# Feed-forward joins of a two-block fp32 kernel: longer tails in token halves, three tile pairs in halves, transposes ahead of the last run

## The reference

```python
h = h + rms_norm(mixed, mix_post_g)                 # mixed = (...) @ w_out          -> "out1"
u = rms_norm(h, ffn_pre_g)                          #                                -> x2
gt, up = split(u @ w_ffn_in)                        # 22 tiles of 128 each           -> g1, u1
h = h + rms_norm((silu(gt) * up) @ w_ffn_out, ffn_post_g)                        #   -> "ffn1"
# second block
x = x + rms_norm(mix @ w_out_2, attn_post_norm)     #                                -> "out2"
h = rms_norm(x, ffn_pre_norm)                       #                                -> x4
x = x + rms_norm(conv_ffn(h, gate, up, ..., down), ffn_post_norm)  # 32 tiles: g2, u2 -> "ffn2"
```

## Time and profile before

| | |
|---|---|
| median of 3 runs | 927.5 us |
| profiled execution | 927.46 us, span 925.7 us |
| TensorE busy | 903.5 us (98%) |
| weight loads, overlapping | 799.8 us (86%) |
| VectorE busy | 678.7 us (73%) |
| ScalarE busy | 465.2 us (50%) |
| GpSimd busy | 222.9 us (24%) |
| granted TensorE clock | full in every slice |

### The profile page before, as it was taken

The page is one execution under the profiler, slowest core; times in us unless marked ns, Lnnn a source line. Parts: engine busy times, 40 slices in busy tenths (PEclk is TensorE's granted clock), DMA queues, the critical chain, the costliest instruction groups (busy, mean ns, idle before and its releaser), DMA issues.

```text
span 925.7 us, 16815 instructions
## 1 busy us (share of the span) xinstructions
PE 903.5 (98%) x6767; PEld 799.8 (86%) x6767; DVE 678.7 (73%) x1274; ACT 465.2 (50%) x936; POOL 222.9 (24%) x120
## 2 busy tenths in 40 slices
PE   8999999999999999999999999999999999999997
PEld 7879999989999888888888799887888888888885
DVE  6924986658655888766676767867888888788885
ACT  6334336564443574434444646776734345544343
POOL 3523421441212211642314342221100211210121
PEclk9999999999999999999999999999999999999999
DMA  8454443234333655655545354224545455455531
GB/s 297 164 188 159 162 142 136 99 113 137 131 122 123 230 178 191 227 183 201 192 160 221 136 190 151 110 90 157 184 153 212 182 182 211 159 222 182 209 110 46
DMA packets 23181, 153.67 MB, mean 166 GB/s; under 512 B 2864, under 2 KB 3248, under 8 KB 5568
## 3 DMA queue, kind: packets, MB, share of 16 engines
q1 hardware_dynamic: 22384, 150.43, 45.9%
q0 software_dynamic: 576, 2.10, 0.6%
q10 hardware_dynamic: 144, 0.07, 0.0%
HBM read 151.28 MB, written 1.05 MB: 165 GB/s over the span
## 4 chain that ended last, share of the span: by engine, by line
PE 61%; DVE 25%; ACT 9%; issue 4%; DMA 0%; DVEq 0%; SPq 0%; ACTq 0%
PE pb L506 59%; DVE wl L515 10%; ACT wh L512 4%; DVE FA L515 4%; DVE FA L521 3%; ACT FA L512 3%; DVE FA L518 3%; PE pb L509 2%; DVE wh L530 1%; ACT R L512 1%; DVE X L521 1%; DVE R L521 1%; DVE st L518 0%; DMA X<-in_x 0%; DVE FA L524 0%
## 5 line engine op out<-in xcount | busy, mean ns | idle before, releaser
L506 PE MATMUL pb<-R,wh 128*128 128x256 f32 (+2 forms) x2224 | 551.5, 327 | 5.9 <-ACT R L512 2.0
L506 PE MATMUL pb<-R,wl 128*128 128x256 f32 (+1 forms) x1512 | 423.9, 282 | 0.0
L506 PEld LDWEIGHTS pb<-R,wh 128*128 128x128 f32 x2224 | 371.9, 189 | 46.4 <-ACT R L512 3.5
L515 POOL TENSOR_TENSOR wl<-raw,wh 128x1024 fp32r<-128x1024 f32 (+1 forms) x80 | 195.0, 2442 | 634.3 <-ACT wh L512 525.1
L515 DVE TENSOR_TENSOR wl<-raw,wh 128x1024 fp32r<-128x1024 f32 (+1 forms) x198 | 263.1, 1350 | 82.4 <-ACT wh L512 80.8
L506 PEld LDWEIGHTS pb<-R,wl 128*128 128x128 f32 x1512 | 286.2, 189 | 2.5 <-issue 0.6
L512 ACT ACTIVATE wh<-raw 128x1024 fp32r<-128x1024 f32 (+1 forms) x219 | 222.7, 1044 | 53.4 <-PE pb L506 51.5
L506 PE MATMUL pb<-wh,R 128*128 128x512 f32 (+2 forms) x724 | 235.0, 389 | 2.3 <-ACT R L512 1.0
L506 PEld LDWEIGHTS pb<-wh,R 128*128 128x128 f32 (+1 forms) x724 | 134.5, 187 | 35.4 <-ACT R L512 2.4
L512 ACT ACTIVATE FA<-pb 128x256 f32<-128x256 f32 (+7 forms) x240 | 94.1, 414 | 127.1 <-PE pb L506 116.0
L506 PE MATMUL pb<-wl,R 128*128 128x512 f32 (+2 forms) x372 | 144.4, 388 | 0.0
(11 more groups left out here) (122 smaller groups left out, 478.5 us busy)
## 6 DMA issues: line engine op xcount, KB each, us to landing
raw<-in_w SPq DMA_DIRECT2D x137, 1024.0 KB, 4.8
X<-in_x SPq DMA_DIRECT2D x2, 512.0 KB, 4.5
raw<-in_w SPq DMA_DIRECT2D x2, 512.0 KB, 6.3
post<-in_ffn_post SPq DMA_DIRECT2D x2, 512.0 KB, 4.5
post<-in_w POOLq DMA_DIRECT2D x2, 512.0 KB, 5.2
FA<-in_w POOLq DMA_DIRECT2D x2, 512.0 KB, 8.6
out<-X SPq DMA_DIRECT2D x4, 256.0 KB, 2.0
cst<-in_cst SPq DMA_DIRECT2D x1, 821.5 KB, 12.0
```

Source lines behind the costliest of these rows:

```text
L506: return self.real.matmul(*a, **k) if self.real else self
L515: return self.real.tensor_tensor(*a, **k) if self.real else self
```

## The change

Six things are changed together:

1. Tails: out1 and out2 sum their last five K blocks in token halves instead of four (`TAIL`). A tail of five runs three blocks for both column halves, then the last two for column half 0, then for column half 1.
2. `SPLIT_TILES` is 3: gate and up tiles 0, 1 and 2 go through `gemm0` and `gemm1`. The third pair takes the banks in `THIRD`.
3. The transposes of token half 0 (`turn`) stand before the tail's last run of half 1, by the new `MIX` strings of out1 and out2.
4. In x2 and x4 the transposes of token half 1 go to two banks, four in each, taken in the order 0, 4, 1, 5, 2, 6, 3, 7; an operand's high part waits for the low part two before it.
5. The wide places begin four units earlier (`opens = first - 4`): 80 to 83 and 176 to 179 are the opened ones. For out2 the splits behind 172 to 174 are issued in the join's own list.
6. `MADE` has other makers for 80, 82, 83, 84, 85, 87, 89 (now d, p, d, d, p, p, q) and 176, 178, 179, 181, 183, 184, 185 (now d, p, d, p, p, q, q).

```diff
-SPLIT_TILES = 2
+SPLIT_TILES = 3
+TAIL = dict(out1=5, ffn1=4, out2=5, ffn2=4)
...
     def down_tail(name, order):
...
-        units = p.weights(("tail", name), [(w, 128 * k, rng(128 * j)) for k in order[-4:] for j in range(8)])
-        return [[("tail", name, c, h)] for c in range(2) for h in range(2)], units
+        n = TAIL[name]
+        units = p.weights(("tail", name), [(w, 128 * k, rng(128 * j)) for k in order[-n:] for j in range(8)])
+        runs = [((0, 1), 0, n - 2), ((0,), n - 2, n), ((1,), n - 2, n)] if n > 4 else [((0,), 0, n), ((1,), 0, n)]
+        return [[("tail", name, c, *r)] for c in range(2) for r in runs], units
...
-        segs.append((down, main, [*chains(down, x), refill(units, list(range(first, first + NWIDE - NBASE)))]))
+        opens = first - (NWIDE - NBASE)
+        held = list(range(units[0] - 8 + TAIL[down], units[0])) if down == "out2" else []
+        segs.append((down, main, [*chains(down, x), refill(held + units, list(range(opens, first)))]))
...
-        return first
+        return opens
...
-MADE = (... "dpddpddvvdddqvddddpd" ... "pvdppvpppdvvdddvpdqddddd" ...)
+MADE = (... "ddddpddpdpqqddddpd" ... "pvdppvppddpddpdpqqqddddd" ...)
...
-    "out1": "............c.cac..aacbab.a.aa..bb.bcbbcc.c...",
+    "out1": "........cccc" "...." ".a.ac.acac.aaa.bbbb......bbbcc......",
...
-    "out2": "c.cac.a.a.aca.bcaa..bbc.bbcbbc....",
+    "out2": "cccccc" "." ".ac.ac.acac.aaa.bbbb......bbbcc......",
...
-        TURN = dict(x2=((4, 5, 0, 1), (6, 7, 4, 5)), x3=((4, 5, 0, 1), (6, 7, 4, 5)), x4=((0, 1, 4, 5), (2, 3, 0, 1)))
+        TURN = dict(x2=((4, 5, 0, 1), (6, 7)), x3=((4, 5, 0, 1), (6, 7, 4, 5)), x4=((0, 1, 4, 5), (2, 3)))
+        THIRD = dict(g1=(4, 5), u1=(4, 5), g2=(0, 1), u2=(0, 1))
...
+        def turns(x, c):
+
+            n = len(TURN[x][c])
+            at = [(k % 4, 128 * (k // 4)) if n == 4 else (k // 4, 128 * (k % 4)) for k in range(8)]
+            return [(k, *at[k]) for k in (range(8) if n == 4 else (0, 4, 1, 5, 2, 6, 3, 7))]
...
                 elif kind == "op":
                     x, c, i = a
-                    for j in range(4):
-                        k = 4 * i + j
+                    for z in range(4 * i, 4 * i + 4):
+                        k, j, at = turns(x, c)[z]
                         e.wait_ge(*pe.at(("turn", x, c, j)))
-                        if i:
-                            e.wait_ge(*dve.at((x, "l", j, c)))
+                        if z >= len(TURN[x][c]):
+                            e.wait_ge(*dve.at((x, "l", turns(x, c)[z - len(TURN[x][c])][0], c)))
```

More of the change, by code:

```diff
@@ L319, in ffn @@
         segs.append((None, p.take(), []))
-        return first
+        return opens
     for n in range(8):
         p.tile("yb", n)
-    for k in range(4):
+    for k in range(8 - TAIL["out1"]):
         p.wide(("down", "out1", k), "w_out", k, [rng(128 * j) for j in range(8)])
@@ L350, in segments @@
         p.tile("mk", n, True)
-    for k in range(4):
+    for k in range(8 - TAIL["out2"]):
         p.wide(("down", "out2", KORD2[k]), "w_out_2", KORD2[k], [rng(128 * j) for j in range(8)])
@@ L433 @@
 for _n, (_, _, _kt) in DOWN.items():
-    _ks = (KORD2 if _n == "out2" else list(range(_kt)))[-4:]
+    _ks = (KORD2 if _n == "out2" else list(range(_kt)))[-TAIL[_n]:]
     TAIL_AT.update({(_n, _k): BLOCK_AT["tail", _n] + 8 * _i for _i, _k in enumerate(_ks)})
@@ L925, in tensor @@
                     src = SRC[name][0]
-                    b = bank(("gemm", name, n), RINGA[name])
+                    b = bank(("gemm", name, n), THIRD[name] if n == 2 else RINGA[name])
                     both = b.rearrange("p (a t) -> p a t", a=2)[:, :, 0:128]
@@ L938, in tensor @@
                     b = banks.of(use)
+                    order = [k for k, _, _ in turns(src, 1)]
                     both = b.rearrange("p (a t) -> p a t", a=2)[:, :, 128:256]
-                    for k in range(8):
+                    for k in order:
                         u, o = divmod(BLOCK_AT["gemm", name, n, 0, 8] + k, 8)
@@ L1014, in tensor @@
                 elif kind == "tail":
[L1015 to L1019, removed]
+                    name, c, hs, k0, k1 = a
+                    ks = (KORD2 if name == "out2" else list(range(DOWN[name][2])))[-TAIL[name]:]
+                    for k in ks[k0:k1]:
+                        m, u = down(name, k, c, False, k == ks[-1], hs)
+                        names = [("used", u), ("down", name, k)] if c and hs[-1] else []
+                        names += [("tail", name, c, h) for h in hs] if k == ks[-1] else []
                         if names:
@@ L1194, in tensor @@
                     m_, = a
-                    b = bank(step, B5, True)
+                    b = bank(step, B4 if m_[0] == "moba" else B5, True)
                     PT, V = Tm(m_), MAPS[m_]["v"]
@@ L1296, in scalar @@
                     x, c, i = a
-                    for j in range(4):
-                        k = 4 * i + j
+                    for z in range(4 * i, 4 * i + 4):
+                        k, j, at = turns(x, c)[z]
                         e.wait_ge(*pe.at(("turn", x, c, j)))
-                        if i:
-                            e.wait_ge(*dve.at((x, "l", j, c)))
-                        e.activation(operand(x, k, 0)[:, 128 * c:128 * c + 128], banks.of(("turn", x, c, j))[:, 128 * i:128 * i + 128],
+                        if z >= len(TURN[x][c]):
+                            e.wait_ge(*dve.at((x, "l", turns(x, c)[z - len(TURN[x][c])][0], c)))
+                        e.activation(operand(x, k, 0)[:, 128 * c:128 * c + 128], banks.of(("turn", x, c, j))[:, at:at + 128],
                                      ACT.Identity, scale=sc(PRE_GAIN[x], k)).then_inc(*act.up((x, "h", k, c)))
@@ L1604, in vector @@
                     x, c, i = a
-                    for j in range(4):
-                        k = 4 * i + j
+                    for z in range(4 * i, 4 * i + 4):
+                        k, j, at = turns(x, c)[z]
                         t = slice(128 * c, 128 * c + 128)
                         e.wait_ge(*act.at((x, "h", k, c)))
-                        e.scalar_tensor_tensor(operand(x, k, 1)[:, t], banks.of(("turn", x, c, j))[:, 128 * i:128 * i + 128],
+                        e.scalar_tensor_tensor(operand(x, k, 1)[:, t], banks.of(("turn", x, c, j))[:, at:at + 128],
                                                sc(PRE_GAIN[x], k), rf(operand(x, k, 0)[:, t]), ALU.mult,
                                                ALU.subtract).then_inc(*dve.up((x, "l", k, c)))
-                        if i:
+                        if z >= 8 - len(TURN[x][c]):
                             banks.ended(("turn", x, c, j), dve.now())
```

15 lines of the change are left out of this document (8 added, 7 removed).

## The result

The changed kernel takes 946.16 us (median of six, 944.89 to 948.03), beside it the kernel before 927.64: ratio 1.0196, 95% interval 1.0185 to 1.0207, so 18.5 us slower. The prediction had 938.4, range 930.0 to 943.5: the direction was right and the time was lost at the three joins it named (A, B and C as there), but the size fell outside the range.

What follows compares the result with a forecast made beforehand. The prediction took TensorE's own work plus its waits to bound the kernel. It added 3.4 (join A), 3.0 (join B) and 4.5 (join C), +10.9, to 927.46 for 938.4 us, range 930.0 to 943.5.

Steps and rivals of the forecast that it cites:

- A: Join from out1 to x2: GpSimd's splits hold VectorE's chain, so half 0's transposes come late; +3.4 us.
- B: Join from ffn1 to x3: splits 158 and 159 move ahead of operand 5, for which TensorE waits; +3.0 us.
- C: Join from out2 to x4: late splits 176 to 179 and GpSimd's turns delay half 0's transposes; +4.5 us.
- Bound: Whole kernel: TensorE is busy 903.5 of 925.7 us, so time is its own work plus its waits.
- The wait for unit 176: Start of join C: the split is ready at 632.8, TensorE wants it at 631.2; stall of 1.6 us.
- The chain held by GpSimd: Join A: 2.3 us GpSimd splits stop X's update and the normalised half; TensorE idles 5.2 us.
- the lower end: All three joins, X's update and norm never held: A 0, C +2.3, B at least 2.5 us.
- R1: Rival: GpSimd's turns fall in VectorE's pauses; A 0, B 3.0, C 2.3, total 932.8 us; chance 0.13.
- The order: Joins A and C: half 1's last run, behind half 0's transposes, covers the first operands; -1.6 us each if transposes start on time.
- R2: Rival: the edit works as worded and is faster; A gains 1.3, C 2.3, total 923.9 us; chance 0.13.
- R3: Rival: TensorE's clock falls after idling; about 0.7 us a join, up to 2; 939.8, up to 942.4 us; chance 0.17.

Runs made afterwards that it cites:

- e4: Changed kernel with the out2 join (join C) put back as in the kernel before: 935.61 us, 8.1 over before.
- e5: Changed kernel plus 26 idle identity transposes ahead of TensorE's wait for normalised half 0 in joins A and C: 944.04 us, 15.4 over before.
- e1: Changed kernel with eleven weight splits of joins A and C taken from GpSimd (ScalarE rounds, VectorE subtracts): 942.83 us, 15.4 over before.
- e3: Changed kernel with the second four operands of x3's token half 1 issued ahead of splits 158 and 159: 942.51 us, 15.0 over before.
- e12: Kernel before with x2's half 0 transposes ahead of out1's last run, half 1's second post step behind the operands: 931.62 us, 3.5 over before.
- e10: Changed kernel, join A's splits off GpSimd and 87 to 89 moved later, x3's operands before splits 158 and 159, join C as before: 931.22 us.
- e7: Changed kernel with one weight split, unit 186, taken from GpSimd (ScalarE rounds, VectorE subtracts): 946.89 us, 18.3 over before.
- e2: Changed kernel with two pairs of gate and up tiles in halves instead of three, in both joins: 948.71 us, 21.2 over before.
- e6: Changed kernel with two tile pairs in halves and half 1 of x2 and x4 transposed into four banks: 945.49 us, 16.9 over before.
- e9: Changed kernel with eleven splits off GpSimd, x3's operands before splits 158 and 159, half 0's chain splits moved later in A and C: 939.58 us.

## Why the prediction was right or wrong

- *Bound.* "TensorE is busy for 903.5 of 925.7 us ... Time is therefore TensorE's own work plus the places where it waits" is the step that failed. It fits the first block (98.4% of the chain from 350 to 515 us). In the second, the folds and e4 show VectorE's chain of hidden steps setting the end of join C, with TensorE nearly level behind it. The chain of waits of before pointed there, and the prediction didn't ask it for this stretch. It left 3.9 us out of the forecast; without these the other misses (1.0, 0.1, 1.4 and 0.7, below) would have left the sum at 941.6, inside the range.
- *Join C, +4.5.* Measured 9.8 (e4: 10.4 by medians). The wait for unit 176 came as forecast (1.37 us). The transposes of half 0 were forecast for 649.6 in the times of the trace before and came at 648.0 and 649.2. TensorE's sum was low by 1.4, no more than the clock's 1.8 (e5). The other 3.9 stood on VectorE between TensorE's end and the first fold, which the sum never reached.
- *Join A, +3.4.* Measured 4.4. Transposes forecast 330.8, measured 331.6, of which 0.7 is the start. The chain held by GpSimd, both turns, is as worked out; the 1.0 more is mostly the clock (0.7 by e5), though the same code costs 4.4 to 5.2 in four traces. What doesn't hold is the lower end, "if X and the norm are never held, A is 0, C is +2.3", and R1 with it: in e1 nothing is held, VectorE makes the low parts itself, and A is 4.7 and C 5.9.
- *Join B, +3.0.* Measured 3.1 and taken away by e3; 4.5 to 4.6 where the clock falls behind it.
- *The order.* "This run then lies over the first operands ... -1.6 us a join, if the transposes start on time" was priced beside the delay of half 1's chain (8.55 us behind half 0's), which was in the sum. In e12 the transposes start on time (328.67) and the gap behind them and the pacing do go (the first tile takes 3.79 us for 4.98), yet A is 3.8 later, some 2 of it at full clock; in e10 they start sooner than before and A costs 3.3. So the condition that the prediction made everything hang on doesn't save the step, and no run supports R2. How much of this the changed kernel's shorter last run (6 matmuls, not 12) would pay at full clock isn't separated.
- *R3, the clock.* It fell as R3 says, and A and C paid 0.7 and 1.8 us, within its "up to 2"; half 1's transposes come 9.3 us (A) and 10.2 (C) behind half 0's instead of 8.55. It left out B and the end, which in some executions pay about 1.5 and 1.6. The rival should have been part of the sum, since the sum itself had TensorE idle for 5 us twice.
- Sum: 10.9 forecast; + 1.0 in A, + 0.1 in B, + 1.4 and + 3.9 in C, + 0.7 at the start = 18.0, against 18.1 at the last fold.

No kernel run here beats the one before; the nearest are e10 and e12, both slower by 0.4%.

## What to carry to other kernels

Ask the chain of waits for each stretch before summing on one engine: an engine that is busy nearly all of a stretch can be the one that is waited for in only 6% of it; then follow the other engine's first and last step too, since the chain's shares change when two engines go level. Where two token halves go through the same serial chain, work that completes half 1's input costs less beside half 0's chain than behind it (e12). And when a sum contains an idle stretch of TensorE, price the clock behind it in the sum, not as a rival.

## What the runs showed of the hardware that was not expected

- The same wait may or may not be followed by the low clock: 2.82 us at B was followed by full clock in the changed kernel, e4 and e7 (B cost 3.1) and by 1.2 GHz in e1, e2, e5 and e6 (4.5 to 4.6); 2.3 us before the last tail by full clock in the changed kernel, e3 and e5 and by 1.2 GHz in e1, e7 and e9. Shorter idling goes both ways too: 1.5 us behind half 0's transposes in join C was followed by full clock in the trace of before and by 1.2 GHz for 3.4 us in e4 and e10, where it cost nothing (the first fold is less than 0.1 us later for it). The changed kernel's six runs go with it: granted clock 0.994 in the three of 944.89 to 945.79 us, 0.987 in that of 948.03.
- GpSimd's subtraction also holds VectorE's X update with a scalar operand (3.52 us for two of 0.71) and the normalising TENSOR_SCALAR with one SBUF tensor (1.99 for 0.49). The Trainium skill (SBUF — State Buffer, Who interferes with whom) has the first by its rule of two SBUF inputs and the second as an operation that can enter a two-port mode; the trace agrees with both.
